# The power of the query and key norm in two halves, and another order of PE and DVE around the first scores, in a float32 hybrid block

## The reference

```python
def hybrid_layer(x, cos, sin, ln1, w_in, ...):
    ...
    mq, mk, mv, sq, sk, sv, xqk, xv, xo, xi, xf = jnp.split(proj, idx, axis=-1)
    mq = apply_rope(rms_norm(heads(mq), moba_q_norm), cos, sin)
    mk = apply_rope(rms_norm(heads(mk), moba_k_norm), cos, sin)
    y_moba = bhsd(moba_attention(bhsd(mq), bhsd(mk), bhsd(heads(mv)))).reshape(B, S, MOBA_WIDTH)
    qk = jax.nn.silu(causal_depthwise_conv(xqk, conv_w, conv_b))
    lq, lk = jnp.split(qk, 2, axis=-1)
    ...
    h = mlstm_chunkwise(bhsd(heads(lq)), bhsd(heads(lk)), bhsd(heads(xv)), i_pre, f_pre)
    ...
    sq = apply_rope(rms_norm(heads(sq), swa_q_norm), cos, sin)
    sk = apply_rope(rms_norm(heads(sk), swa_k_norm), cos, sin)
    y_swa = swa_attention(sq, sk, heads(sv), swa_sinks).reshape(B, S, SWA_Q_WIDTH)
    x = x + jnp.concatenate([y_moba, y_mlstm, y_swa], axis=-1) @ w_out
    u = rms_norm(x, ln2) @ w_up
    return x + jnp.square(jax.nn.relu(u)) @ w_down
```

## Time and profile before

| what | value |
|---|---|
| median of 3 runs (lowest to highest) | 1818.23 us (1817.28 to 1818.33) |
| the profiled execution: its time, its span | 1818.69 us, 1816.9 us |
| mean granted clock of PE | 0.996 |
| PE busy | 1769.9 us, 97% of the span |
| DVE, ACT, POOL busy | 1148.8, 950.3, 44.4 us |
| PE's share of the chain that ended last | 90% |

### The profile page before, as it was taken

How to read it: one execution, slowest core, us unless ns; L and a number is a source line. 1 busy time by engine, 2 the same in 40 slices (tenths; PEclk the granted TensorE clock), 3 DMA queues, 4 the chain that set the end, 5 groups by cost and what they waited for, 6 DMA issues and landing times.

```text
span 1816.9 us, 23998 instructions
## 1 busy us (share of the span) xinstructions
PE 1769.9 (97%) x9920; PEld 1460.5 (80%) x9920; DVE 1148.8 (63%) x1351; ACT 950.3 (52%) x1286; POOL 44.4 (2%) x32
## 2 busy tenths in 40 slices
PE   7899999989999999999999999999999999999998
PEld 6768888777888889777888897688888787778887
DVE  5776555586755665477656755677556655776555
ACT  6464555545545554465445644656455546654443
POOL 0100000010000000000000000000000000000000
PEclk9999999999999999999999999999999999999999
DMA  8465555745556565755655556537555756355552
GB/s 272 139 232 163 186 189 194 243 139 203 192 189 194 195 222 197 233 179 169 223 194 185 186 175 203 192 115 242 186 186 186 231 167 227 103 176 171 195 190 70
DMA packets 226003, 342.07 MB, mean 188 GB/s; under 512 B 7684, under 2 KB 116584, under 8 KB 225896
## 3 DMA queue, kind: packets, MB, share of 16 engines
q1 hardware_dynamic: 225080, 339.27, 56.4%
q10 hardware_dynamic: 816, 1.28, 0.2%
HBM read 339.48 MB, written 1.05 MB: 187 GB/s over the span
## 4 chain that ended last, share of the span: by engine, by line
PE 90%; DVE 4%; ACT 3%; issue 1%; POOL 1%; DMA 0%; SPq 0%; DVEq 0%; POOLq 0%; ACTq 0%
PE PS L1872 15%; PE PS L1873 15%; PE PS L1874 15%; PE PS L1926 14%; PE PS L1927 7%; PE PS L1914 2%; PE PS L1916 2%; PE PS L1915 2%; PE PS L2254 1%; PE PS L1958 1%; PE PS L2312 1%; PE PS L2256 1%; PE PS L2255 1%; PE PS L2335 1%; PE PS L2323 1%
## 5 line engine op out<-in xcount | busy, mean ns | idle before, releaser
L1164 DVE TENSOR_TENSOR LO<-RAW,HI 128x2048 fp32r<-128x2048 f32 (+1 forms) x272 | 619.8, 2290 | 294.6 <-ACT HI L648 293.5
L648 ACT CAST HI<-RAW 128x2048 fp32r<-128x2048 f32 (+1 forms) x272 | 517.6, 1909 | 162.5 <-PE PS L1874 129.8
L1926 PE MATMUL PS<-AHL,HI 128*128 128x512 f32 x1120 | 396.2, 398 | 0.0
L1927 PE MATMUL PS<-AHL,LO 128*128 128x256 f32 x1120 | 314.3, 281 | 0.0
L1926 PEld LDWEIGHTS PS<-AHL,HI 128*128 128x128 f32 x1120 | 210.4, 188 | 51.9
L1872 PE MATMUL PS<-HI,HIDH 128*128 128x512 f32 x640 | 250.1, 391 | 0.0
L1873 PE MATMUL PS<-LO,HIDH 128*128 128x512 f32 x640 | 249.2, 389 | 0.0
L1874 PE MATMUL PS<-HI,HIDL 128*128 128x512 f32 x640 | 249.1, 389 | 0.0
L1872 PE MATMUL PS<-HI,AHL 128*128 128x512 f32 (+2 forms) x672 | 245.7, 366 | 0.0
L1873 PE MATMUL PS<-LO,AHL 128*128 128x512 f32 (+2 forms) x672 | 240.3, 358 | 0.0
L1874 PE MATMUL PS<-HI,AHL 128*128 128x512 f32 (+2 forms) x672 | 240.3, 358 | 0.0
(11 more groups left out here) (286 smaller groups left out, 2226.4 us busy)
## 6 DMA issues: line engine op xcount, KB each, us to landing
RAW<-in_w_ff SPq DMA_DIRECT2D x96, 1024.0 KB, 5.3
RAW<-in_w_in SPq DMA_DIRECT2D x78, 1024.0 KB, 5.2
RAW<-in_w_mod SPq DMA_DIRECT2D x48, 1024.0 KB, 5.1
RAW<-in_w_up SPq DMA_DIRECT2D x32, 1024.0 KB, 5.4
RAW<-in_w_down SPq DMA_DIRECT2D x32, 1024.0 KB, 5.0
RAW<-in_w_o SPq DMA_DIRECT2D x12, 1024.0 KB, 5.0
RAW<-in_w_out SPq DMA_DIRECT2D x8, 1024.0 KB, 7.0
RAW<-in_w_attn_out SPq DMA_DIRECT2D x6, 1024.0 KB, 5.0
```

The source lines that it names most:

```text
L648: return nc.scalar.copy(dst, src)
L1164: tt(LO[:, c % RAW_N, 0:n], RAW[:, c % RAW_N, 0:n], HI[:, NTH[c] % HL_N, 0:n].bitcast(F32), ALU.subtract).then_inc(s_lo, 1)
L1926: mm(PS[:, b + q, :], wh, AHL[:, j, :, :].rearrange("p a n -> p (a n)"), start=j == 0, stop=False)
L1927: ins = mm(PS[:, b + q, 0:256], wl, AH[:, j, :], start=False, stop=j == KT - 1)
```

## The change

It has five parts. The reordered stage is run twice, in layer 0 and layer 1.

1. **The opening.** The 16 transposes of the very first norm go to banks 4 to 7 (`norm_bank`) and no longer wait for the split of earlier ones.
2. **The power.** POOL does the 24 numbers as two instructions of 12, one a token tile; DVE's multiplication is split likewise, and the first half waits only for the first power (`s_rs0`).
3. **DVE's splits.** The split of c0 + 9 moves from behind `weigh` to in front of it, that of c0 + 10 from behind `probabilities(0)` to behind `weigh`. `weigh` goes in plain order and signals once.
4. **The banks.** Turned queries and keys of the first two steps go to banks 2 and 3, not 6 and 7.
5. **PE's order.** The first tile of c0 + 8 goes in front of the mLSTM's scores, its second tile in front of `turn_qk(0)`; the tiles of c0 + 9 and c0 + 10 move up one place each; `turn(1)`, `scores(2)`, `values(0)` and `turn_weights(2)` now stand behind the first tile of c0 + 10.

```diff
-QT_BANK = (0, 1, 0, 0, 1, 0)
+QT_BANK = (2, 3, 6, 6, 7, 6)
...
+        def norm_bank(n, s):
+
+            return 4 + s if n == 0 else 6 + s % 2
...
-                for j, width in enumerate((2, 24, 2 * (NQK - 12), 8, 2)):
-                    rsqrt(5 * l + j, width)
+                rsqrt(5 * l, 2)
+                pool.wait_ge(s_ms, 5 * l + 2)
+                nc.gpsimd.tensor_tensor(RS[:, 0:12], MS[:, 0:12], NHALF[:, 0:12], ALU.pow).then_inc(s_rs0, 1)
+                nc.gpsimd.tensor_tensor(RS[:, 12:24], MS[:, 12:24], NHALF[:, 0:12], ALU.pow).then_inc(s_rs, 1)
...
-                    dve.wait_ge(s_rs, 5 * l + 2 + r)
...
-                    link(tt(q, z, rs.to_broadcast((P, NT, n, DH)), ALU.mult))
+                    if r == 0:
+                        dve.wait_ge(s_rs0, l + 1)
+                        tt(q[:, 0, :, :], z[:, 0, :, :], rs[:, 0, :, :].to_broadcast((P, n, DH)), ALU.mult)
+                        dve.wait_ge(s_rs, 5 * l + 2)
+                        link(tt(q[:, 1, :, :], z[:, 1, :, :], rs[:, 1, :, :].to_broadcast((P, n, DH)), ALU.mult))
...
                 qk_cos(0)
+                ahead(c0 + 6)
...
                 weigh()
-                ahead(c0 + 6)
+                ahead(c0 + 7)
                 maxima(0)
                 maxima(1)
                 probabilities(0)
-                ahead(c0 + 7)
...
-                    pe.wait_ge(s_tlo, n + s + 1)
+                    if n:
+                        pe.wait_ge(s_tlo, n + s + 1)
...
+                pe.wait_ge(s_gfree, g0 + 5)
+                half_tile(c0 + 8, 0, 0, 0)
...
-                pe.wait_ge(s_gfree, g0 + 5)
-                half_tile(c0 + 8, 0, 0, 0)
-                pe.wait_ge(s_mp, 2 * l + 1)
+                half_tile(c0 + 8, 0, 0, 1)
+                pe.wait_ge(s_gfree, g0 + 6)
                 pe.wait_ge(s_qk, 2 * l + 1)
                 turn_qk(0)
                 turn_qk(1)
-                half_tile(c0 + 8, 0, 0, 1)
+                half_tile(c0 + 9, 0, 1, 0)
                 pe.wait_ge(s_qtc, 6 * l + 2 + 2)
-                pe.wait_ge(s_mp, 2 * l + 2)
+                pe.wait_ge(s_mp, l + 1)
                 scores(0)
                 turn_qk(2)
-                pe.wait_ge(s_gfree, g0 + 6)
                 turn_weights(0)
-                half_tile(c0 + 9, 0, 1, 0)
+                half_tile(c0 + 9, 0, 1, 1)
                 pe.wait_ge(s_qtc, 6 * l + 3 + 2)
                 scores(1)
                 turn(0)
                 turn_weights(1)
-                half_tile(c0 + 9, 0, 1, 1)
+                pe.wait_ge(s_gfree, g0 + 7)
+                tokens_out(c0 + 10, 0, KT, 256, AH, AL, True, True, tiles=(0,))
                 turn(1)
                 scores(2)
                 values(0)
                 turn_weights(2)
-                pe.wait_ge(s_gfree, g0 + 7)
-                tokens_out(c0 + 10, 0, KT, 256, AH, AL, True, True, tiles=(0,))
+                tokens_out(c0 + 10, 0, KT, 256, AH, AL, True, True, tiles=(1,))
                 turn(2)
                 values(1)
-                tokens_out(c0 + 10, 0, KT, 256, AH, AL, True, True, tiles=(1,))
-                values(2)
                 pe.wait_ge(s_mtc, 3 * l + 3)
                 modulation(0)
+                values(2)
                 modulation(1)
```

More of the change, by code:

```diff
@@ L362, in build @@
         s_rs = sem("rstd_done")
+        s_rs0 = sem("rstd_first_tile")
         s_src = sem("transpose_source")
@@ L629, in _ @@
             for l in range(DEPTH):
-                for j, width in enumerate((2, 24, 2 * (NQK - 12), 8, 2)):
-                    rsqrt(5 * l + j, width)
+                rsqrt(5 * l, 2)
+                pool.wait_ge(s_ms, 5 * l + 2)
+                nc.gpsimd.tensor_tensor(RS[:, 0:12], MS[:, 0:12], NHALF[:, 0:12], ALU.pow).then_inc(s_rs0, 1)
+                nc.gpsimd.tensor_tensor(RS[:, 12:24], MS[:, 12:24], NHALF[:, 0:12], ALU.pow).then_inc(s_rs, 1)
+                rsqrt(5 * l + 2, 2 * (NQK - 12))
+                rsqrt(5 * l + 3, 8)
+                rsqrt(5 * l + 4, 2)
             pool.wait_ge(s_src, SRC1 * DEPTH - 1)
@@ L709, in high @@
                     if scale is None:
-                        cast(dst, PS[:, 6 + s % 2, :].rearrange("p (a n) -> p a n", a=2)).then_inc(s_thi, 1)
+                        cast(dst, PS[:, norm_bank(n, s), :].rearrange("p (a n) -> p a n", a=2)).then_inc(s_thi, 1)
                         continue
@@ L716, in high @@
                         last = nc.scalar.activation(out[:, j, :],
-                                                    PS[:, 6 + s % 2, 256 * j:256 * j + 256], ACT.Identity,
+                                                    PS[:, norm_bank(n, s), 256 * j:256 * j + 256], ACT.Identity,
                                                     scale=scale(2 * s + j),
@@ L848, in turned @@
                     cast(QKT[:, 2 * j:2 * j + w // 256, :].rearrange("p a n -> p (a n)"),
-                         PS[:, 6 + QT_BANK[j], 0:w]).then_inc(s_qtc, 1)
+                         PS[:, QT_BANK[j], 0:w]).then_inc(s_qtc, 1)
                 def weights_turned(j):
@@ L1187, in low @@
                     dve.wait_ge(s_thi, n + s - steps[0] + 1)
-                    full = PS[:, 6 + s % 2, :] if scale is None else TMP[:, s % 2, :]
+                    full = PS[:, norm_bank(n, s), :] if scale is None else TMP[:, s % 2, :]
                     full = full.rearrange("p (a n) -> p a n", a=2)
@@ L1191, in low @@
                         for j in range(2):
-                            last = ts(TMP[:, s % 2, 256 * j:256 * j + 256], PS[:, 6 + s % 2, 256 * j:256 * j + 256],
+                            last = ts(TMP[:, s % 2, 256 * j:256 * j + 256], PS[:, norm_bank(n, s), 256 * j:256 * j + 256],
                                       scale(d + j), shift(d + j), ALU.mult, ALU.add)
@@ L1196, in low @@
                         for j in range(2):
-                            last = stt(lo[:, j, :], PS[:, 6 + s % 2, 256 * j:256 * j + 256], scale(d + j), hi[:, j, :],
+                            last = stt(lo[:, j, :], PS[:, norm_bank(n, s), 256 * j:256 * j + 256], scale(d + j), hi[:, j, :],
                                        ALU.mult, ALU.subtract)
@@ L1344, in qk_norm @@
                     q, z, n, gains = parts(r)
-                    dve.wait_ge(s_rs, 5 * l + 2 + r)
                     rs = RS[:, 0:2 * n].rearrange("p (t h) -> p t h", t=NT).unsqueeze(3)
-                    link(tt(q, z, rs.to_broadcast((P, NT, n, DH)), ALU.mult))
+                    if r == 0:
[3 more added lines that the diff above has]
+                        link(tt(q[:, 1, :, :], z[:, 1, :, :], rs[:, 1, :, :].to_broadcast((P, n, DH)), ALU.mult))
+                    else:
+                        dve.wait_ge(s_rs, 5 * l + 3)
+                        link(tt(q, z, rs.to_broadcast((P, NT, n, DH)), ALU.mult))
                     for i, (h1, h2) in enumerate(gains):
@@ L1441, in weigh @@
                     dve.wait_ge(s_ms3, l + 1)
-                    for j in (2, 0, 1):
+                    for j in range(3):
                         for b in range(2):
@@ L1447, in weigh @@
                                        ISC, m, ALU.mult, ALU.mult)
-                        if j != 0:
-                            last.then_inc(s_mp, 1)
+                    last.then_inc(s_mp, 1)
                 def invert(h1, n):
@@ L1830, in transposes @@
                             col = 128 * (2 * (s + first) + k)
-                            last = nc.tensor.transpose(PS[:, 6 + (s + first) % 2, 256 * k + 128 * t:256 * k + 128 * t + 128],
+                            last = nc.tensor.transpose(PS[:, norm_bank(n, s + first), 256 * k + 128 * t:256 * k + 128 * t + 128],
                                                        src[:, t, col:col + 128], IDM)
@@ L2048, in turn_qk @@
                             last = nc.tensor.transpose(
-                                PS[:, 6 + QT_BANK[j], 256 * k + 128 * t:256 * k + 128 * t + 128],
+                                PS[:, QT_BANK[j], 256 * k + 128 * t:256 * k + 128 * t + 128],
                                 QK[:, t, h:h + 2, :].rearrange("p h d -> p (h d)"), IDM)
```

## The result

The changed kernel takes 1824.55 us (median of 6 runs, 1821.65 to 1826.7), the kernel before 1817.99 (1817.28 to 1818.47): a ratio of 1.0034, interval 1.0024 to 1.0044. It is slower by 6.6 us, and outside the range of the prediction (1814.0 to 1822.5).

A forecast was written before the change was run, and what follows sets the result against it. The prediction took PE, busy 97% of the span, as the bound. Layer 0 (-0.9 + 0.33), layer 1 (-0.45 + 0.33) and the opening (-0.2) gave -0.9 us together: 1818.23 becomes 1817.3 us, range 1814.0 to 1822.5.

The forecast's parts named there:

- the one that left the clock at full level: PE behind the new 3.9 us stall: forecast has no clock loss; rival, clock falls in one or both layers, 0.34.
- The rival's price for one fall: PE's clock falling in the new stall: 2.1 us a fall, between 1.6 and 2.9; chance of falls 0.34.
- the power's term: POOL's power in two halves, each layer: rotation's end 0.33 us later, between 0.49 earlier and 0.33 later.
- The chain on PE: PE from the rotation's end to the mLSTM's products: waits of 1.5, 1.4 and 3.6 to 3.9 us, 30.8 in all.
- The sum against before: Rotation's end to the mLSTM's products: 30.8 us against 31.69 and 31.25, so 0.9 and 0.45 less in layers 0 and 1.
- R: The end of DVE's rotation of queries and keys, where the weighing begins; at 74.92 us in layer 0 before.
- POOL held up by the multiplication, R + 0.33: DVE's first half multiplication holds up POOL's second power, so the rotation ends 0.33 us later in each layer.
- the rival without contention: POOL's second power isn't held up: rotation ends 0.49 us earlier, 1815.7 us in all; chance 0.16 with clock whole.
- The opening, -0.2: First norm's transposes without waits for DVE: 0.2 us gained, between 0 and 0.3, ending at the forget gates' products.
- The copy not late, 1809.5: Rival: ACT's copy of c0 + 9 isn't late, 3.9 us come back in each layer, 1809.5 us; chance 0.09.

The follow-up runs named there:

- e4: The changed kernel with seven unread products on PE ahead of the wait for the copy of c0 + 9: 1823.58 us, ratio 1.0029.
- e2: The kernel before with only the opening's part of the change: 1818.15 us, ratio 1.0000.
- e5: The changed kernel with unread products ahead of three waits of PE (gates, transposes, copy of c0 + 9): 1818.64 us, ratio 1.0002.
- e10: e3 with 4.05 us of unread products in PE's old stall ahead of the transposes: 1813.26 us, ratio 0.9974.
- e6: The changed kernel with ACT's copy of c0 + 9 moved ahead of the second pair's exponentials: 1811.6 us, ratio 0.9965.
- e7: e6 with the opening's transposes as in the kernel before: 1808.43 us, ratio 0.9951.
- e3: The kernel before with only the power and its multiplication in halves: 1816.6 us, ratio 0.9993.
- e11: e7 with the power whole again: 1809.63 us, ratio 0.9957.

## Why the prediction was wrong

**The failed step is the one that left the clock at full level**, "In one layer that gives 1819.4, in both 1821.5, up to 1823" with a chance of 0.34, beside a forecast whose sum had no term for it. The prediction had the mechanism as a rival, and its ground against it, "only stalls of 4.9 us are known to have ended low", was the weak place. The runs showed falls behind waits of 3.6 and 2.7 us, and behind two of 1.2 and 1.0 us with only the transposes between them. The rival's price for one fall, 2.1 us (1.6 to 2.9), was if anything too high: 3.4 us of low clock cost 1.5 to 1.6 us. What it missed is how often the clock falls: after lost 1.5 in layer 0, but 4.0 in layer 1 with its 10.2 us of low clock, and up to 1.7 to 2 at the gates (first power at 61.42 against 59.67 in e4 and 59.43 in e2, which have the same opening; 0.3 to 0.5 of that was there when the gates' products began). Without these losses the profiled execution's 1823.69 us would be 1816.2 to 1816.5; e5's profiled execution gives 1817.4, less the 2.6 by which its own fill put the gates off. Both are estimates, and with the power's term put right the prediction's own sum would be 1815.7: without the clock the change would have been a small gain or none.

Point by point:

- *The chain on PE* was right. Transposes at the rotation's end with a wait of 1.2 us (predicted 1.5), the tile of c0 + 9 with 1.0 (1.4), the tile of c0 + 10 with 3.61 (3.6 to 3.9), released by the copy of Z. From the rotation's end to the mLSTM's products it is 30.48 us at full clock (30.8). In after's layer 0 it is 108.19 - 76.20 = 31.99, with the low clock in it, and the gain of 0.9 against the old 31.69 was gone.
- *The sum against before.* The prediction set R + 30.8 at full clock against 31.69 and 31.25, which have low clock in them. At full clock the old order takes 28.90 (e10) and the new one 30.48, so the 0.9 was no gain of the order. At full clock the stage is 58.0 against 59.67 and 59.22, a gain of 1.7 and 1.2. But the kernel before had 6.8 us of low clock in each of these stages, so against it even the longer order gains as long as its own clock stays up. The change gave up one wait of 4.9 us and took three of 5.8; what it could win was only the low clock behind the old one, and it brought low clock of its own.
- *POOL held up by the multiplication, R + 0.33*: the sign was wrong. That "POOL stands still while such an instruction of DVE runs" was read rightly for the splits: the first half power ended at 65.67, which is the predicted 63.94 and the 1.73 by which everything came later. It was wrong to carry it over to the multiplication, which had no row: the second power took 2.27 us beside it, undisturbed. R came 0.45 earlier against the power's start (76.20 - 61.42 against 74.92 - 59.69), as the rival without contention had it (0.49). The contention that the Trainium skill tells of (GPSIMD Engine Reference, the table at its head) is seen here for the splits (6.15 us in place of an estimated 4.16) and not for this multiplication, which has two inputs in SBUF as well.
- *The opening, -0.2*: right where the first products run at the lower level (e2: -0.26), wrong where they run at the higher one, since then PE's lead turns into 2.7 us of waiting and the clock falls. The prediction said that the gates are bound by the parameter rows and stopped there; it did not ask what PE does with the time that it gains.
- *The copy not late, 1809.5*: the change didn't do it, but the size was right (3.9 us a layer). e6 did it with one moved statement and came to 1811.6, e7 to 1808.4.

What stays open: why the first products run at one level or the other under the same code, why a split holds POOL up and a multiplication doesn't, and which of the three waits in a layer makes the clock fall in a given execution (e7 has the two short ones and kept it in its profile; one of its five runs took 1812.1 us at 0.998).

## What to carry to other kernels

When an edit moves a wait, add up all waits of the busiest engine before and after, and price the clock behind each new one: 3.4 us of low clock cost 1.6 us here (e3 against e10, and one layer against the other in e4 and in e11). A wait for a copy is best looked for on the copying engine: what stood ahead of it on ACT was itself waiting, and moving the copy into that wait gave 3.9 us a layer at full clock, the power's halves 0.5. And fill a wait with idle products as a test, not only as a cure: it tells clock from chain in one run, if the fill is shorter than the wait.

## What the hardware showed that I had not expected

- Behind waits of 3.6 and 2.7 us the granted clock was as low as 0.56 and 0.69, and in layer 1 of after it fell at gaps of 1.2 and 1.0 us (0.70 from 405 to 410 us).
- The first products of the kernel run at 0.22 or at 0.12 us for 264 columns in different executions of the same code, while the granted clock reads 1.00 in both.
- POOL's power of n numbers takes 0.39 + 0.157 n us. Under a split it ends that time less 0.12 to 0.15 us behind the split, even when it started 0.9 us ahead of it beside a memset; under a multiplication of two tensors it isn't held up at all.
